# A hybrid attention block on one core: band bias and maximum per head in one operation, group A's row maxima placed by a DMA, and new order offsets

## What is computed

```python
logits = logits - sl[...] * dist                       # ALiBi
p = jax.nn.softmax(jnp.concatenate([logits, sink], axis=-1), axis=-1)[..., :-1]
```

## Time and profile before

| | |
|---|---|
| median of three runs | 1547.6 us (1540.68 to 1549.32) |
| profiled execution, its own time | 1548.81 us |
| its span in the trace | 1547.0 us |
| mean granted TensorE clock | 0.968 of full speed |
| chain that ended last, by engine | PE 61%, DVE 17%, issue 9%, ACT 7%, POOL 3%, DMA 3% |

### The profile page before, as it was taken

How to read it: one execution, slowest core, us unless ns; L and a number is a source line. 1 busy time by engine, 2 the same in 40 slices (tenths; PEclk the granted TensorE clock), 3 DMA queues, 4 the chain that set the end, 5 groups by cost and what they waited for, 6 DMA issues and landing times.

```text
span 1547.0 us, 19248 instructions
## 1 busy us (share of the span) xinstructions
PE 1419.2 (92%) x6520; PEld 1031.9 (67%) x6520; DVE 1194.9 (77%) x2235; ACT 932.4 (60%) x1797; POOL 420.6 (27%) x268
## 2 busy tenths in 40 slices
PE   5998999899999985797999989999999999989997
PEld 4887888678887764465556646556565764468886
DVE  3377878879988966989999998999998770047776
ACT  3285875975963888557969756787995734301010
POOL 3332222752334324304021120121212601012321
PEclk9999999999999996899899999999999999999999
DMA  6322221431325235311222230222214412034442
GB/s 226 108 83 90 82 83 65 164 123 41 110 82 131 91 97 122 93 49 40 62 72 66 64 93 11 60 59 60 65 41 128 128 35 68 0 116 139 147 149 82
DMA packets 104305, 136.34 MB, mean 88 GB/s; under 512 B 6498, under 2 KB 81126, under 8 KB 103950
## 3 DMA queue, kind: packets, MB, share of 16 engines
q1 hardware_dynamic: 91344, 93.16, 21.9%
q10 hardware_dynamic: 9216, 31.20, 5.2%
q0 software_dynamic: 3648, 10.76, 2.2%
HBM read 92.76 MB, written 42.34 MB: 87 GB/s over the span
## 4 chain that ended last, share of the span: by engine, by line
PE 61%; DVE 17%; issue 9%; ACT 7%; POOL 3%; DMA 3%; SPq 0%; ACTq 0%; POOLq 0%; DVEq 0%
PE psum L1200 18%; PE psum L1389 9%; PE psum L1343 9%; PE psum L1271 4%; DVE above L1484 3%; ACT above L1029 3%; PE psum L1330 3%; PE psum L1332 3%; PE psum L1331 3%; DVE score L1512 2%; PE psum L1216 2%; PE psum L1231 2%; POOL w_lo L852 2%; PE psum L1233 2%; DVE dist L1515 1%
## 5 line engine op out<-in xcount | busy, mean ns | idle before, releaser
L1484 DVE TENSOR_SCALAR_CACHE_REDUCE above<-dist,trial 128x512 bf16<-128x512 int32 (+13 forms) x224 | 346.0, 1544 | 6.1
L1029 ACT ACTIVATE above<-dist,trial 128x384 bf16<-128x384 int32 (+13 forms) x224 | 280.9, 1254 | 45.4 <-DVE trial L1457 28.8
L1200 PE MATMUL psum<-x_hi,w_hi 128*128 128x512 f32 x640 | 254.0, 397 | 36.7 <-POOL w_lo L852 28.6
L1343 PE MATMUL psum<-prob,vw 128*65 128x512 f32 x544 | 269.2, 596 | 0.0
L1139 ACT ACTIVATE prob<-psum 128x512 f32<-128x512 f32 x272 | 158.5, 592 | 159.5 <-PE psum L1343 142.0
L1200 PE MATMUL psum<-x_lo,w_hi 128*128 128x512 f32 x640 | 251.7, 393 | 0.0
L1200 PE MATMUL psum<-x_hi,w_lo 128*128 128x512 f32 x640 | 251.6, 393 | 0.0
L1581 DVE CUSTOM_DVE_ANT_0 junk<-psum,mask 128x512 bf16<-128x512 f32 (+3 forms) x320 | 184.1, 606 | 23.9 <-PE psum L1274 13.0
L1200 PEld LDWEIGHTS psum<-x_hi,w_hi 128*128 128x128 f32 x640 | 121.8, 190 | 68.6 <-POOL w_lo L852 33.7
L1331 PE MATMUL psum<-qa_mix,ka_mix 128*128 128x512 f32 x272 | 161.4, 593 | 0.0
L1271 PE MATMUL psum<-ka_ext,qa_ext 128*128 128x512 f32 (+3 forms) x320 | 136.7, 468 | 19.3 <-DVE part_max L1581 10.5
(11 more groups left out here) (154 smaller groups left out, 2834.4 us busy)
## 6 DMA issues: line engine op xcount, KB each, us to landing
raw<-w_tiles SPq DMA_DIRECT2D x40, 512.0 KB, 4.1
proj<-staged ACTq DMA_DIRECT2D x40, 512.0 KB, 3.5
qb_raw<-proj SPq DMA_DIRECT2D x32, 256.0 KB, 4.1
qa_raw<-proj SPq DMA_DIRECT2D x32, 256.0 KB, 4.5
yt_raw<-y_t SPq DMA_DIRECT2D x16, 512.0 KB, 5.2
x_row<-x_res SPq DMA_DIRECT2D x16, 512.0 KB, 3.9
out<-z ACTq DMA_DIRECT2D x16, 512.0 KB, 2.6
x_raw<-xT SPq DMA_DIRECT2D x12, 512.0 KB, 4.3
```

Of the source, the lines that this page charges most:

```text
L1029: nc.scalar.activation(above[:, 0, 0:n], src, ACT.Sign, scale=-1.0, bias=u, accum_out=count[:, 0:1]).then_inc(sign_counted, 1)
L1200: last = pe.matmul(psum[:, 2 * u + m, :], wt[:, u, k, :], xt[:, k, 512 * m:512 * m + 512], start=(k == 0 and q == 0), stop=(k == KT - 1 an ...
L1343: pe.matmul(psum[0:65, 6 + g, :], vw[:, kt, 0:65], prob[:, u % 3, :], start=(kt == 0), stop=(kt == b)).then_inc(a_used, 1)
L1484: v.tensor_scalar(above[:, 1, 0:n], src, u, None, ALU.is_ge, ALU.add, accum_out=count[:, 1:2]).then_inc(own_counted, 1)
```

## The change

1. `bias_b`: instead of one addition over four heads and one maximum over four heads, one add-and-maximum operation per head; the sink logit enters as the operation's starting scalar. The wait between the two is gone.
2. Row maxima of group A: `scan_max` writes its maximum straight into `row_top` for b < 4; for b >= 4 `top_of_chunks` reduces over chunks. `turn_max` (PE) transposes, `leave_max` (DVE) negates 8 x 128 elements into `minus_max`, and `place_max`, a DMA issued by SP, writes them as one row of 1024 into `qa_ext`. `negate`, `row_max`, `sel`, `load_sel` and the ACT copies of `sel` go. The next block's scan waits for `leave_max`, no longer for the placing.
3. `y_a_of`: one reciprocal and one multiplication instead of two each.
4. DVE's `setup_pieces` no longer waits for the stored tiles; the first `scan_max` and the first gate loads do.
5. The planner: new durations for several pieces, new delays, new offsets in all of `PREFER`, so a new order of pieces on every engine.

```diff
-AFTER = {"load_w": 3.6, "load_x": 3.4, ... "load_sel": 3.0,
+AFTER = {"load_w": 2.6, "load_x": 3.2, ... "place_max": 2.4,
-PREFER = {'window': 109.7, 'den_b': 5.7, 'scan': 1188.4, ...
+PREFER = {'window': 1442.6, 'den_b': 920.6, 'scan': 2751.2, ...
...
-            add("DVE", 0.2 + 1.0 * w / 512, "sum", *part,
+            add("DVE", 0.25 + 1.05 * w / 512, "sum", *part,
-        add("SP", 0.35, "load_x", m, ...
+        add("SP", 1.35, "load_x", m, ...
-        add("SP", 0.35, "load_w", half, t, ...
-        add("POOL", 1.05, "round_w", half, t, ...
-        add("POOL", 2.42, "split_w", half, t, ...
+        add("SP", 1.35, "load_w", half, t, ...
+        add("POOL", 1.3, "round_w", half, t, ...
+        add("POOL", 2.6, "split_w", half, t, ...
...
-            add("DVE", 1.95 if b else 1.3, "bias_b", b, g,
+            add("DVE", 1.5 if b else 1.2, "bias_b", b, g,
...
-        add("DVE", 0.35, "negate", b, needs=[scan_list[-1]])
-        add("PE", 0.11, "minus_max", b, needs=[("negate", b)])
-        add("DVE", 1.25, "row_max", b, needs=[("minus_max", b), ("setup_act",), ("positions", b)])
+        if b >= 4:
+            add("DVE", 0.25, "top_of_chunks", b, needs=[scan_list[-1]])
+        add("PE", 0.11, "turn_max", b, needs=[scan_list[-1], ("top_of_chunks", b)])
+        add("DVE", 0.3, "leave_max", b, needs=[("turn_max", b), ("place_max", b - 1)])
+        add("SP", 0.4, "place_max", b, needs=[("leave_max", b), ("positions", b)])
...
-        add("DVE", 1.2, "y_a", b, needs=[("turn_a", b), ("columns_a", b - 1)])
+        add("DVE", 1.0, "y_a", b, needs=[("turn_a", b), ("columns_a", b - 1)])
...
+            def place_max(b):
+                sp.wait_ge(a_left_max, b + 1)
+                sp.dma_start(qa_ext[HD:HD + 1, b % 2, :, :].rearrange("p h q -> p (h q)").bitcast(F32),
+                             minus_max[:, :].bitcast(F32)) \
+                    .then_inc(a_ext, 16)
...
@@ scan_logits @@
-                        pe.wait_ge(a_ext, b)
+                        pe.wait_ge(a_left_max, b)
@@ unit_logits @@
-                    pe.wait_ge(a_ext, b + 1)
+                    pe.wait_ge(a_ext, 16 * (b + 1))
...
-                v.tensor_tensor(two(lb, HD), ps, two(bias, 0), ALU.add).then_inc(b_biased, 1)
-                dve.wait_ge(b_biased, 2 * b + g + 1)
-                small(v.tensor_reduce(mb[:, hs], lb[:, hs, HD + j0:HD + WIN + 1], AX_X, ALU.max))
+                for i in range(4):
+                    h = 4 * g + i
+                    last = v.tensor_tensor_reduce(out=lb[:, h, HD + j0:HD + WIN],
+                                                  in0=psum[:, 2 + i // 2, WIN * (i % 2) + j0:WIN * (i % 2) + WIN],
+                                                  in1=bias[:, h, j0:WIN], scale=1.0, scalar=sink8[:, h:h + 1],
+                                                  op0=ALU.add, op1=ALU.max, accum_out=mb[:, h:h + 1])
+                last.then_inc(b_biased, 1)
...
-            def negate(b):
...
-                v.tensor_tensor(qa_ext[HD:HD + H, s, :, :], psum[0:H, 0, 0:P].unsqueeze(1).broadcast_to([H, H, P]),
-                                sel[:, :, :], ALU.mult).then_inc(a_ext, 1)
+            def top_of_chunks(b):
                 dve.wait_ge(a_scanned, scans_to(b))
+                v.tensor_reduce(row_top[:, 0:H], part_max[:, :, 0:1 + b // 4], AX_X, ALU.max).then_inc(a_top, 1)
+
+            def leave_max(b):
+                dve.wait_ge(a_turned_max, b + 1)
+                if b:
+                    dve.wait_ge(a_ext, 16 * b)
+                v.tensor_scalar(minus_max[:, :], psum[0:H, 0, 0:P], -1.0, None, ALU.mult).then_inc(a_left_max, 1)
...
-                for g in range(2):
-                    last = v.reciprocal(rec_a[:, 4 * g:4 * g + 4], heads[g][:, :, HD])
-                last.then_inc(a_rec, 1)
+                v.reciprocal(rec, heads[:, :, :, HD]).then_inc(a_rec, 1)
```

More of the change, by code:

```diff
@@ L82 @@
                    "copy_b", "mix_b", "y_b", "columns_b", "gate_b"),
-          "scan": ("load_qa", "round_qa", "split_qa", "positions", "scan", "scan_max", "negate", "minus_max", "row_max"),
+          "scan": ("load_qa", "round_qa", "split_qa", "positions", "scan", "scan_max", "top_of_chunks", "turn_max", "leave_max", "place_max"),
           "units": ("logits", "exp_a", "values", "leave_a"),
@@ L223, in tile @@
             two = tiles[n - 2]
-        add("SP", 0.35, "load_w", half, t, needs=[("split_w", *two)] if n >= 2 else [])
-        add("POOL", 1.05, "round_w", half, t, needs=[("load_w", half, t)] + ([("product", *two, KT - 1)] if n >= 2 else []))
-        add("POOL", 2.42, "split_w", half, t, needs=[("round_w", half, t)])
+        add("SP", 1.35, "load_w", half, t, needs=[("split_w", *two)] if n >= 2 else [])
+        add("POOL", 1.3, "round_w", half, t, needs=[("load_w", half, t)] + ([("product", *two, KT - 1)] if n >= 2 else []))
+        add("POOL", 2.6, "split_w", half, t, needs=[("round_w", half, t)])
     def products(half, t, k):
@@ L298, in whole_plan @@
     add("POOL", 3.2, "extra_rows", needs=[end])
-    add("SP", 0.7, "load_sel", needs=[end, ("store", 1, N_TILES - 1), ("store", 1, N_TILES - 2)])
-    add("ACT", 1.7, "setup_act", needs=[("load_sel",)])
-    add("DVE", 1.8, "setup_dve", needs=[end, ("store", 1, N_TILES - 1), ("store", 1, N_TILES - 2)])
+    add("ACT", 1.0, "setup_act", needs=[end])
+    add("DVE", 1.8, "setup_dve", needs=[end])
     add("ACT", 0.25, "put_sink", 0, needs=[("setup_dve",)])
+    stores = [("store", 1, N_TILES - 1), ("store", 1, N_TILES - 2)]
     last_values = lambda b: ("values", b, b, 1)
@@ L779, in load_gate_a @@
                 else:
-                    sp.wait_ge(setup_act, 1)
+                    for i in range(2):
+                        sp.wait_ge(stored[i], 16 * N_TILES)
                 load_gate(gate_a, ROW_G, b, gate_a_in)
@@ L786, in load_gate_b @@
                 else:
-                    sp.wait_ge(setup_act, 1)
+                    sp.wait_ge(tile_mm, 2 * N_TILES)
+                    for i in range(2):
+                        sp.wait_ge(stored[i], 16 * N_TILES)
                 load_gate(gate_b, ROW_G + 4 * P, b, gate_b_in)
@@ L1538, in setup_pieces @@
                 dve.wait_ge(tile_mm, 2 * N_TILES)
-                for i in range(2):
-                    dve.wait_ge(stored[i], 16 * N_TILES)
                 v.memset(mask[:, 0, 0:P], 0.0)
@@ L1577, in scan_max @@
                 w = min(512, n_keys - c)
+                if scan == 0:
+                    for i in range(2):
+                        dve.wait_ge(stored[i], 16 * N_TILES)
                 dve.wait_ge(a_scan, scan + 1)
@@ L1637, in y_a_of @@
                     dve.wait_ge(a_yt, b)
-                for g in range(2):
-                    last = v.tensor_tensor(y_a[:, 4 * g:4 * g + 4, :], heads[g][:, :, 0:HD],
-                                           rec_a[:, 4 * g:4 * g + 4].unsqueeze(2).broadcast_to([P, 4, HD]),
-                                           ALU.mult)
-                last.then_inc(a_y, 1)
+                v.tensor_tensor(y_a[:, :, :].rearrange("p (g h) d -> p g h d", g=2), heads[:, :, :, 0:HD],
+                                rec.unsqueeze(3).broadcast_to([P, 2, 4, HD]), ALU.mult).then_inc(a_y, 1)
             run_order(order, {
```

92 lines of the change are left out of this document (38 added, 54 removed).

## The result

The changed kernel took 1555.35 us (median of 5 runs, 1554.56 to 1558.48) against 1545.26 us for the kernel before, run beside it: a ratio of 1.0065 with a 95% interval of 1.0049 to 1.0081. It is slower by 10 us. The forecast was 1521 us, faster, and its range ended at 1549.

A forecast was written before the change was run, and what follows sets the result against it. Nearly balanced PE and DVE, waiting on each other between 572.6 and 1192 us, were taken as the bound. 1548.8 - 22 (DVE) - 4 (start) + 3 (placing) - 4 (order) = 1521.8, stated as 1521 us; range 1497 to 1549.

The forecast's parts named there:

- The order: New order on all engines: 4 us gained from the projection's w_lo waits and a better mesh later; ends 15 us either way.
- The slower one: Rival: row maxima placed late by SP or the DMA in the attention stage, about 1570 us; chance 0.10.
- I take 22 us, a little over half: Attention stretch, 572.6 to 1192 us: of 39 us freed on DVE, 22 us become time; ends 0 and 39.
- 39 + 6.6 us: DVE work saved: 39 us between 572.6 and 1192 us, 6.6 us behind it beside a full PE, worth nothing.
- The 4 us for the start of the stage: Attention start: DVE's 7.87 us wait for the last stored tile is used for search steps, 4 us gained; ends 0 and 7.9.
- Rival (a): PE takes over as bound, so lighter DVE work gains little: 1540 to 1550 us; chance 0.12.
- The placing: Row maxima by SP's DMA, in place 1.5 to 3.5 us later before each block's first logits: 3 us lost; ends 0 and 26.
- With the old order the delay would cost 7 us at 1.5 us: Blocks' first logits waiting for the placed row, order unchanged: 7 us lost at 1.5 us delay, 26 us at 3.5 us.
- Rival (b): The row maxima's placing is late, through SP's queue or a 4.0 us DMA: about 1570 us; chance 0.10.
- The durations: DVE's four bias-and-maximum operations start 0.28 us apart, 1.20 us a group instead of 1.99, saving 0.79 us.
- Rival (c): The four bias operations cost their full duration, 1.73 us a group; DVE gains 25 us, time about 1531 us; chance 0.10.
- DVE's total: Sign of being right: DVE's busy time over the whole kernel falls from 1194.9 to about 1150 us.

The follow-up runs named there:

- late_wait: New operations, new order up to the projection's last product, old order behind, PE's wait for the placed row two matmuls later; 1533.13 us, 0.9913 of the kernel before.
- after_late_wait: The changed kernel with PE's wait for the placed row moved behind the two matmuls that don't read it; 1556.17 us, 1.0063 of the kernel before.
- the two halves: New operations, new projection order; attention order new only up to search 6's masks (1550.74 us, 1.0027) or only behind them (1563.71 us, 1.0105).
- the two edits on the search: Last search spread over 85 more pieces in the changed kernel (1621.25 us, 1.0482); drawn together by 85 in the old order with new operations (1606.27 us, 1.0382).
- new_ops_old_order: All new operations in the order of the kernel before, with its planner, durations and offsets; 1542.83 us, 0.9987 of the kernel before.
- the late wait: New operations in the old order, PE's wait for the placed row moved behind two matmuls that don't read it; 1537.51 us, 0.9942 of the kernel before.

## Why the prediction was wrong

The runs give a sum in which every step is a difference of two ratios, times 1545 us; each is uncertain by some 3 to 5 us, as the intervals are:

| step | predicted, us | measured, us | from |
|---|---|---|---|
| lighter operations, placing mostly hidden | -22, and -4 for the start | -9 | 1.0000 to 0.9942 |
| order, projection | -4 (with the rest of the order) | -4.5 | 0.9942 to 0.9913 |
| order, attention stage (placing hidden) | nothing of its own | +23 | 0.9913 to 1.0063 |
| placing, in the new order | +3 | 0 | 1.0063 to 1.0065 |
| sum | -27 | +10 | 1.0065 |

The table goes one way through the runs. With the wait left where the changed kernel has it, the operations and the placing together are worth -2 us (0.9987), the order -4 us in the projection and +16 us in the attention stage: the 7 us between +16 and +23 are the placing's, which the new order hides anyway.

**The order** is the step that failed and turned the sign: taken as a gain of 4 us, it is a loss of 12 us as it stands (18 us where the placing is hidden). It read "I take 4 us from them and from a better mesh later. Ends: 15 us gained, 15 us lost". The 4 us came from a row (w_lo's waits beyond the first tile) and are the right number for the stage that this row is of, the projection, but partly by luck: nearly half of the earlier end of that stage (4.5 of 9.7 us) lies ahead of the first product, which the prediction had set aside, and w_lo's other waits (12.2 us, now 3.5) were largely replaced by those for `staged` (1.3 us, now 9.9). For the attention stage no row was used; it went in at nothing, and it was 16 to 23 us. A warning was in the text: in a stretch where PE and DVE are busy at 89% and 91%, who comes first can be worth as much as any operation. The order's own end of 15 us lost covers the 12, but alone it leads to 1541 us only, and none of the rivals had the order as the reason for a slower kernel. The slower one was the placing.

How these 23 us show is clear from the windows of `late_wait`, which has the old attention order, beside those of `after_late_wait`, which has the new one and the same wait. The attention stage of `late_wait`:

```profile
565.80:1339.60 773.80, 708.09 (x3262) 447.14 (x3261) 598.36 (x1455) 539.68 (x1024) 178.22 (x125) 0.95 0.26 68
```

In `after_late_wait` it takes 795.7 us. PE is busy 708.1 us instead of 719.7 and idle 65.7 us instead of 76.0. So half of the order's cost is a longer busy time for the same work, more of which runs at the lower clock, and half is gaps. Two stretches of `late_wait`, then the same of `after_late_wait`:

```profile
750.00:900.00 150.00, 143.84 (x711) 91.84 (x711) 136.96 (x347) 119.00 (x238) 33.73 (x26) 1.00 0.24 60
900.00:1100.00 200.00, 190.33 (x890) 120.60 (x888) 178.35 (x415) 147.96 (x272) 34.76 (x27) 0.98 0.23 61
```

```profile
750.00:900.00 150.00, 133.81 (x637) 84.22 (x635) 141.61 (x320) 117.93 (x234) 30.18 (x24) 0.96 0.23 63
900.00:1100.00 200.00, 185.14 (x882) 120.00 (x883) 184.18 (x438) 158.12 (x298) 33.31 (x25) 0.96 0.21 56
```

PE is idle 15 us more between 750 and 1100 us, at clocks of 0.96 instead of 1.00 and 0.98. Ahead of 750 us the new order is the better one (PE busy 87% from about 600 to 750 us, against 82%). So the loss lies in the middle of the stage, while the prediction had looked for its gain mostly ahead of 750 us. Which pieces of the new order make the gaps is not shown: the two halves don't add, and the two edits on the search broke more than they tested. That the search ends earlier is what the windows show; that this is the cause is only argued.

**"I take 22 us, a little over half"** failed too. DVE's freed time in the attention stage was forecast at 39 + 6.6 us; it is 35 us (625.3 to 590.0 in the old order). Of this 2 us became time, and 9 us, about a quarter, once the wait for the placing was moved. PE's waits for DVE were named as a measure (27 us), and in `new_ops_old_order` they did fall, to 15 us (between 572 and 1185 us):

```profile
PE psum L1378 <- DVE y_a L1651: 5.8, 2, 5.4
PE psum L1286 <- DVE part_max L1604: 4.8, 6, 3.0
PE psum L1378 <- DVE y_b L1631: 4.0, 2, 2.7
```

But 9.9 us of waits for the placing took their place, and much of DVE's freed time became waiting for PE (10.1 to 19.7 us for the scans). The 4 us for the start of the stage went the same way: DVE's wait of 7.9 us for the stored tile is gone, its first scans wait 11.6 us for PE instead of 4.0 (570 to 610 us), and PE is busy 14.0 us of the stage's first 32.4 us instead of 13.5. Rival (a), in which PE takes over and a lighter DVE is worth little, is nearest to this: it gave 1540 to 1550 us, and the same operations in the old order took 1542.8. It had a chance of 0.12. Its working was off, though: it had PE's waits fall by 7% and the start give its 4 us, so that the number fits is partly luck. And it says nothing of the 10 us that the changed kernel lost.

This error is as large as the order's: operations, start and placing together were forecast at 23 us gained and gave 2, the order at 4 us gained and cost 12. Either error alone would still have left a faster kernel.

**The placing** was read rightly in kind. "With the old order the delay would cost 7 us at 1.5 us": the late wait gives back 7 us in the old order. That the two are equal is luck, since PE still waits 6.2 us for the placing behind the late wait, and five placings took 1.8 to 3.9 us to land (last section). "The planner now counts 2.4 us for it and can put scans or another block's values in between": PE waits 1.3 us in the new order, and `after_late_wait` gives back nothing. Rival (b) is out. SP does wait for `leave_max` at the head of its queue, 143 us in all, but the loads behind it are not late for PE: at the first scans it waits 2.5 us for qa_mix (5.7 before) and at the bands 1.8 us for qb_mix (0.9 before).

```profile
SPq L775 <- DVE minus_max L1607: 143.3, 13, 47.9
```

**The durations** were nearly right, and here the estimate from the Trainium skill came nearer than the one from the rows. The four operations were taken at 0.28 us each, start to start; they are 0.34 us, so a group saves 0.64 us (1.99 to 1.35), not 0.79. The estimate from the fixed cost on the page "VectorE: DVE Perf Modes" of the Trainium skill was 1.4 us a group, and the measurement of 1.35 us is near it. The slope of 1.04 ns a column, drawn through the scan's operation, is right: back to back the new operation starts 0.27 us apart at 128 columns and 0.34 us at 192. What was missed is a fixed part: at 128 columns the scan's operation starts 0.21 us apart in the same trace, so the new one costs 0.06 us more each. (By the page's fixed cost the scan's would be 0.29 us, so that cost of the Trainium skill fits the one operation, start to start, and not the other.) It differs in that it writes float32 and not bf16 and starts from a tensor's scalar and not a constant; which of these costs the time is not shown. Rival (c), 1.73 us a group, is farther off. The whole bias part is worth 3.7 us by itself, so neither size would have turned the result.

**DVE's total** was forecast at about 1150 us; in the old order it is 1159.3, and 1143.3 in the new one. The other 16 us are not the change's operations but the order, in the projection and in the attention stage about alike: with the new order in the projection alone the total is 1153.4 us, with it in the attention stage alone 1151.0 (next section but one).

## What to carry to other kernels

In a kernel whose engines run orders written out ahead, price a shorter operation with that order held fixed: where two engines are nearly balanced, at most a quarter of the saving came back here, while time added at one of the same places cost three quarters. Price a re-planned order as a change of its own, stage by stage, with a range from both sides that is as wide as PE's idle and slow-clock time in that stage, and test it by running the old order with the new operations. And when an operand comes late by DMA, wait for it directly ahead of the first instruction that reads it: that single line was worth 7 us where the order left no room for the delay, and nothing where it did.

## What the hardware showed that was not expected

The same instruction on DVE has two durations, depending on POOL. Groups of DVE by form in the kernel before (count, busy us, mean ns):

```profile
L1448 DVE TENSOR_TENSOR score<-score,dist 128x3072 int32<-128x3072 int32 x1 | 5.4, 5377 | 0.0
L1448 DVE TENSOR_TENSOR score<-score,dist 128x2560 int32<-128x2560 int32 x1 | 2.8, 2827 | 0.0
```

and the first of them in the changed kernel, on the same shape:

```profile
L1457 DVE TENSOR_TENSOR score<-score,dist 128x3072 int32<-128x3072 int32 x1 | 3.4, 3360 | 0.0
```

In the kernel before it started at 495.40 us, while POOL was in an operation on w_lo that ended at 497.55, and took 2.0 us longer: about what was left of POOL's operation. In the changed kernel POOL did nothing from 494.7 to 504.0 us. POOL pays as well: `w_lo` has a median of 2.40 us in both kernels and a longest of 4.75 us before, 3.17 us after.

```profile
L852 POOL TENSOR_TENSOR w_lo<-raw,w_hi x40: 2345/2403/4751, 14.0 to 552.2; 128x1024 fp32r<-128x1024 f32 x40
```

```profile
L858 POOL TENSOR_TENSOR w_lo<-raw,w_hi x40: 2342/2404/3170, 7.1 to 542.4; 128x1024 fp32r<-128x1024 f32 x40
```

The Trainium skill ("SBUF — State Buffer", on the shared port pair) says that a DVE operation with two inputs in SBUF and a GpSimd operation that reads SBUF exclude each other for a whole instruction; both rows agree. It is not only the large operations that stand so. `nmb`, one input of 8 columns, has a minimum of 0.16 us and took 1.95 us where it started beside a POOL operation (`qa_mix`, 628.62 to 630.98 us):

```profile
629.07 1.95 DVE L1568 TENSOR_SCALAR nmb<-mb 128x8 f32<-128x8 f32 x1
```

This makes busy time depend on the order. Summed over all of DVE's instructions, the time above the shortest of the same form is 14 us less in the changed kernel than in `new_ops_old_order` for those that overlap a POOL instruction, and 1 us less for the others: that is nearly all of the 16 us by which DVE's total fell further. Whether it also shortened the projection was not measured.

The placing: SP needs 0.69 us to issue it, where 0.4 us were assumed. On the chain of `new_ops_old_order` its 4 KB take from 1.82 to 3.93 us to land, as wide a spread as the 96 KB loads of the earlier trace rows had, so its size does not make it quick.

```profile
613.00 1.82 DMA qa_ext<-minus_max
...
738.24 3.93 DMA qa_ext<-minus_max
```
